# Seven half products in place of eight on a quarter of the depth, in six of the FFN's eleven pairs of blocks

## The reference, cut to what matters

```python
def swiglu(h, w_ffn_in, w_ffn_out):
    gate, up = jnp.split(h @ w_ffn_in, 2, axis=-1)     # h: 256 x 2048, w_ffn_in: 2048 x 11264
    return (jax.nn.silu(gate) * up) @ w_ffn_out         # w_ffn_out: 5632 x 2048

h = rms_norm(x, norm2_gain[l]) * (1 + scale2) + shift2
x = x + gate2 * swiglu(h, w_ffn_in[l], w_ffn_out[l])
```

## Time and profile before

| | |
|---|---|
| median of 3 runs | 3428.91 us |
| profiled execution, whole | 3425.8 us |
| its span, first to last instruction | 3424.1 us |
| mean granted clock of TensorE | 0.875 of full |
| busy over the span | PE 76%, DVE 73%, ACT 25%, POOL 32% |

### The profile page before, as it was taken

One profiled execution on the slowest core, in us unless ns is written; L12 is line 12 of the kernel. 1 busy time (PEld: TensorE's weight loads), 2 busy tenths in 40 slices (PEclk: granted clock), 3 DMA queues, 4 the chain that ended last, 5 costly groups with the idle time before them and its releaser, 6 DMA issues. The chain is left out here.

```text
span 3424.1 us, 27357 instructions
## 1 busy us (share of the span) xinstructions
PE 2587.7 (76%) x10431; PEld 1805.0 (53%) x10431; DVE 2513.7 (73%) x2615; ACT 860.9 (25%) x815; POOL 1102.7 (32%) x654
## 2 busy tenths in 40 slices
PE   9999999616051500035558999999999999999999
PEld 4455774202020200012226888788788788888887
DVE  5987657899999999976776876779566544444565
ACT  2113331100000110000003333455433433333333
POOL 6640007686777688876660000000000000000000
PEclk9999999757575755567779999999999999999999
DMA  8885569999999999999997997455657555555775
GB/s 287 320 315 205 183 243 406 403 422 419 422 421 417 409 420 422 422 421 421 422 421 260 327 323 260 145 162 166 221 185 252 167 194 184 192 187 188 269 266 185
DMA packets 317685, 1023.39 MB, mean 299 GB/s; under 512 B 33656, under 2 KB 34184, under 8 KB 250892
## 3 DMA queue, kind: packets, MB, share of 16 engines
q1 hardware_dynamic: 243676, 484.97, 41.2%
q0 software_dynamic: 73904, 537.04, 37.9%
HBM read 1015.08 MB, written 6.86 MB: 298 GB/s over the span
## 5 line engine op out<-in xcount | busy, mean ns | idle before, releaser
L411 DVE TENSOR_TENSOR slab_low<-ring,slab_high 128x2048 fp32r<-128x2048 f32 x220 | 504.2, 2292 | 488.3 <-ACT slab_high L404 488.2
L404 ACT CAST slab_high<-ring 128x2048 fp32r<-128x2048 f32 x284 | 542.3, 1910 | 890.8 <-PE bank L390 714.7
L2137 POOL DMA_INDIRECT pool<-in_peer_u,pool x237 | 493.8, 2084 | 293.5 <-DVE pool L1861 185.9
L1911 DVE CUSTOM_DVE_ANT_0 pool<-pool,nat 128x2048 f32<-128x2048 f32 x234 | 532.7, 2291 | 45.7 <-DMA pool<-in_peer_u,pool 44.2
L388 PE MATMUL bank<-slab_high,left_high 128*128 128x512 f32 x1408 | 551.3, 392 | 8.4 <-DVE res L1949 3.9
L390 PE MATMUL bank<-slab_high,left_low 128*128 128x512 f32 x1408 | 549.0, 390 | 0.0
L389 PE MATMUL bank<-slab_low,left_high 128*128 128x512 f32 x1408 | 548.8, 390 | 0.0
L2710 PE MATMUL bank<-pool,causal 128*128 128x512 f32 x296 | 181.5, 770 | 415.7 <-ACT causal L2352 325.4
L1922 DVE SCALAR_TENSOR_TENSOR res<-pool,res 128x2048 f32<-128x2048 f32 x169 | 397.4, 2351 | 105.9 <-DMA pool<-in_peer_v,pool 92.5
L2137 POOL DMA_INDIRECT pool<-in_peer_v,pool x242 | 394.9, 1632 | 214.0 <-PE bank L2710 107.7
L2710 PE MATMUL bank<-pool,upto 128*128 128x512 f32 x288 | 195.9, 844 | 209.2 <-DMA pool<-in_peer_v,pool 116.3
(11 more groups left out here) (661 smaller groups left out, 3466.1 us busy)
## 6 DMA issues: line engine op xcount, KB each, us to landing
ring<-in_w_in SPq DMA_DIRECT2D x140, 1024.0 KB, 5.2
ring<-in_w_ffn_in SPq DMA_DIRECT2D x88, 1024.0 KB, 5.0
ring<-in_w_ffn_out SPq DMA_DIRECT2D x44, 1024.0 KB, 5.2
nat<-in_w_ada SPq DMA_DIRECT2D x74, 512.0 KB, 5.8
ring<-in_w_out SPq DMA_DIRECT2D x32, 1024.0 KB, 5.1
ring<-in_w_ada SPq DMA_DIRECT2D x28, 1024.0 KB, 6.7
left_scratch<-in_w_ada SPq DMA_DIRECT2D x38, 512.0 KB, 5.7
pool<-in_w_ada SPq DMA_DIRECT2D x12, 1024.0 KB, 7.1
```

Of the source, the lines that this page charges most:

```text
L404: nc.scalar.copy(high[:, n % PARTS], ring[:, g % SLOTS]).then_inc(high_done, 1)
L411: eng.tensor_tensor(dst, ring[:, g % SLOTS], high[:, n % PARTS].bitcast(F32), ALU.subtract)\
L1911: v.tensor_tensor_reduce(out=row, in0=row, in1=nat[:, t, :], scale=1.0, scalar=0.0, op0=ALU.mult, op1=ALU.add, accum_out=actv[:, t, m:m + ...
L2137: g.indirect_dma_start(dst, None, a[table][0], bass.IndirectOffsetOnAxis(idx[:, t, n:n + 1], 0))\
```

## The change

It applies to pairs 1 to 6 (`SEVEN`). Of each of these pairs, depth quarter 3 (slab (0, 3) of the gate and slab (1, 3) of the up block) is multiplied by Winograd's form of Strassen's scheme. The 2 x 2 blocks are: tokens t x halves of that depth quarter on the left (2 chunks each, `HK`), depth halves x gate/up on the right. Eight half products (6 matmuls each) become seven. The other six slabs (`rest`, r = 0 to 5) stay as before.

- **Left sums, once.** POOL makes four sums of the left's blocks from the normed rows (`left_sums`, 128x256 each); PE transposes them in pair 0 before slab 5 (8 transposes), ACT and DVE split them.
- **Right sums, in each pair.** DVE adds halves of the two slabs in place in the ring (`slab_sum`, four of 128x1024). The parts that PE multiplies are cast and split by halves: FIRST, SECOND, THIRD (two halves each) and FOURTH (one half), seven halves in place of eight, from slots 0 and 1.
- **Order of PE in a pair.** rest 0, FIRST (12 matmuls), rest 1, SECOND (12), hidden transposes, rest 2, THIRD (12), rest 3, FOURTH (6), rest 4, rest 5.
- **Parts.** A third pair of part buffers is laid over the end of `hTh`, which pairs 1 to 6 don't reach. Buffers in that order: 2, 0, 1, 2, 0, 1, 2, 1, 0, 1. FOURTH's cast so waits for THIRD's products, rest 5's for FOURTH's.
- **Banks.** Banks 6 and 7 hold three of the half products in turn. ACT copies FIRST's and SECOND's out (`take`); DVE forms the common sums (`one_and_six`, `with_seventh`, `five_less`), adds them to banks 0 and 1 (`seven_gates`) and 2 and 3 (`seven_ups`). Silu now reads `prod_` in place, after `seven_gates` and after the cast of rest 5 in ACT's queue. Banks 0 and 1 are free for the next pair once `seven_gates` is done.
- **Loads.** Slots 0 and 1 hold the two summed slabs until THIRD's and FOURTH's low parts are made; the loads of rest 4 and rest 5 wait for these. The next pair's first loads stand behind them in SP's queue.
- Some semaphores of the norms are shared, to make room for six new ones; pair 1 is no longer written out by itself.

The diff, cut to its core:

```diff
+        SEVEN, HK = range(1, 7), KS // 2
+        SEVEN_PART = (0, 2, 1, 1)
+        SEVEN_FROM = (((0, 0), (0, 1)), ((1, 1), (0, 0)), ((1, 1), (0, 1)), ((1, 0),))
+        REST_AT, REST_PART, rest_count = (2, 3, 6, 7, 4, 5), (2, 1, 0, 2, 0, 1), (3, 1, 1, 1, 1, 1)
 sync:
-                stream(sp, FFN_IN)
+                ffn_loads()
+                def seven_loads(i):
...
+                    else:
+                        for at, after, p, j in ((2, 5, 0, 0), (3, 6, 0, 1), (0, 7, 0, 3), (1, 8, 1, 3)):
+                            sp.wait_ge(low_done, before + after)
+                            ffn_load(i, at, p, j)
+                    for r in (2, 3):
+                        sp.wait_ge(low_done, before + 8 + r + 1)
+                        ffn_load(i, REST_AT[r], r // 3, r % 3)
+                    for r, last in ((4, THIRD), (5, FOURTH)):
+                        sp.wait_ge(s_wl, i * 4 - 4 + last + 1)
+                        ffn_load(i, REST_AT[r], r // 3, r % 3)
 tensor:
+                def half_product(n, which, lhs, bank, start, stop):
+                    hi, lo = part_pair(SEVEN_PART[n])
+                    for k in range(HK):
+                        lh, ll = lhs(k)
+                        c = HK * which + k
+                        nc.tensor.matmul(ps[bank][:, :], lh, hi[:, c, :], start=start and k == 0, stop=False)
+                        nc.tensor.matmul(ps[bank][:, :], lh, lo[:, c, :], start=False, stop=False)
+                        last = nc.tensor.matmul(ps[bank][:, :], ll, hi[:, c, :], start=False, stop=stop and k == HK - 1)
+                def seven_pair(i, first):
...
+                        pe.wait_ge(s_wd, i * 6 - 7)
+                    rest(i, 0)
+                    pe.wait_ge(s_wl, i * 4 - 3)
+                    half_product(FIRST, 0, own(0, 0), 6, True, True)
+                    half_product(FIRST, 1, own(1, 0), 0, False, False).then_inc(s_wu, 1)
+                    rest(i, 1)
...
+                        pe.wait_ge(s_wd, i * 6 - 6)
+                    pe.wait_ge(s_wl, i * 4 - 2)
+                    half_product(SECOND, 0, summed(3), 2, True, False)
+                    half_product(SECOND, 1, summed(0), 7, True, True).then_inc(s_wu, 1)
...
+                    hidden_transposes(i)
+                    rest(i, 2)
+                    pe.wait_ge(s_wl, i * 4 - 1)
+                    pe.wait_ge(s_wx, i * 2 - 1)
+                    half_product(THIRD, 0, summed(1), 6, True, True)
+                    half_product(THIRD, 1, own(1, 1), 1, False, True).then_inc(s_wu, 1)
+                    rest(i, 3)
+                    pe.wait_ge(s_wl, i * 4 + 0)
+                    pe.wait_ge(s_wx, i * 2 + 0)
+                    half_product(FOURTH, 0, summed(2), 7, True, True).then_inc(s_wu, 1)
+                    rest(i, 4)
+                    rest(i, 5)
 scalar:
+                def seven_silu(i):
+                    act.wait_ge(s_wd, i * 6 - 1)
+                    for t in range(TT):
+                        last = nc.scalar.activation(prod_[:, t, :], prod_[:, t, :], ACT.Silu)
+                    last.then_inc(s_fa, 1)
+                def seven_pair(i, first):
+                    rest_high(i, 0, first)
+                    seven_high(i, FIRST)
+                    rest_high(i, 1)
+                    seven_high(i, SECOND)
+                    rest_high(i, 2)
+                    take(i, FIRST, 6, taken_one)
+                    highs(i - 1)
+                    seven_high(i, THIRD)
+                    rest_high(i, 3)
+                    act.wait_ge(s_fu, i * 1)
+                    take(i, SECOND, 7, taken_five)
+                    seven_high(i, FOURTH)
+                    rest_high(i, 4)
+                    rest_high(i, 5)
+                    seven_silu(i)
 vector:
+                def five_less(i):
+                    dve.wait_ge(s_wx, i * 2 + 0)
+                    dve.wait_ge(s_wd, i * 6 - 4)
+                    v.tensor_tensor(taken_six, taken_five, taken_six, ALU.subtract).then_inc(s_wd, 1)
+                    v.tensor_tensor(taken_five, taken_five, taken_last, ALU.subtract).then_inc(s_wd, 1)
+                def seven_gates(i):
+                    dve.wait_ge(slabs_used, i * 8 + (gf + 5))
+                    dve.wait_ge(s_fT, i * 1)
+                    v.tensor_tensor(prod_[:, 0, :], ps[0][:, :], taken_one, ALU.add)
+                    v.tensor_tensor(prod_[:, 1, :], ps[1][:, :], taken_last, ALU.add).then_inc(s_wd, 1)
+                def seven_pair(i, first):
+                    rest_low(i, 0)
+                    seven_low(i, FIRST)
+                    slab_sum(i, 0, (0, 0), (1, 0))
+                    if first:
+                        product(i - 1)
+                    else:
+                        seven_ups(i - 1)
+                    rest_low(i, 1)
+                    slab_sum(i, 1, (1, 0), (1, 1))
+                    if not first:
+                        seven_product(i - 1)
+                    seven_low(i, SECOND)
+                    slab_sum(i, 2, (1, 1), (0, 0))
+                    slab_sum(i, 3, (0, 1), (1, 1))
+                    rest_low(i, 2)
+                    lows(i - 1)
+                    seven_low(i, THIRD)
+                    rest_low(i, 3)
+                    one_and_six(i)
+                    seven_low(i, FOURTH)
+                    rest_low(i, 4)
+                    with_seventh(i)
+                    rest_low(i, 5)
+                    five_less(i)
+                    seven_gates(i)
```

More of the change, by code:

```diff
@@ L3548, in _, with left_sum_transposes @@
             @block.tensor
             def _(pe):
+                def left_sum_transposes():
+                    pe.wait_ge(s_ws, 4)
+                    pe.wait_ge(s_nl, len(low_order))
+                    for q in range(4):
+                        for j in range(HK):
+                            c = (q % 2 * HK + j) * P
+                            last = nc.tensor.transpose(ps[6 + q // 2][:, c:c + P], summed_rows[q][:, j * P:(j + 1) * P],
+                                                       ident[:, :])
+                    last.then_inc(s_nT, 1)
@@ new lines, in rest @@
+                def rest(i, r):
+                    p, j = divmod(r, 3)
+                    pe.wait_ge(low_done, i * 8 + (nf + sum(rest_count[:r + 1])))
+                    hi, lo = part_pair(REST_PART[r])
+                    for k in range(KS):
+                        for t in range(TT):
+                            lh, ll = left(KS * j + k, t)
+                            o = ps[2 * p + t][:, :]
+                            begin = j == 0 and k == 0 and (p, t) != (1, 0)
+                            end = j == 2 and k == KS - 1 and (p, t) != (0, 1)
+                            nc.tensor.matmul(o, lh, hi[:, k, :], start=begin, stop=False)
+                            nc.tensor.matmul(o, lh, lo[:, k, :], start=False, stop=False)
+                            last = nc.tensor.matmul(o, ll, hi[:, k, :], start=False, stop=end)
+                    last.then_inc(slabs_used, rest_count[r])
@@ L3618, in last_products, with pair @@
                                          j == 0, j == 3)
-                def pair(i, first, second=False):
+                def pair(i, first):
                     for p in range(2):
@@ L3623, in pair @@
                             m = 4 * p + j
+                            if first and p == 1 and j == 1:
+                                left_sum_transposes()
                             if first and p == 0 and j < WHOLE:
@@ L3684, in _ @@
                 pair(0, True)
-                pair(1, False, True)
-                with pe.Fori(2, pairs) as i:
+                seven_pair(SEVEN.start, True)
+                with pe.Fori(SEVEN.start + 1, SEVEN.stop) as i:
+                    seven_pair(i, False)
+                with pe.Fori(SEVEN.stop, pairs) as i:
                     pair(i, False)
@@ L3742, in silu @@
                         act.wait_ge(s_fT, i * 1)
+                    else:
+                        act.wait_ge(s_ws, 2)
                     for t in range(TT):
@@ L3751, in highs, with left_sum_highs, seven_high @@
                     last.then_inc(s_fh, 1)
+                def left_sum_highs():
+                    act.wait_ge(s_nT, len(turn_order) + 1)
+                    for h in range(2):
+                        nc.scalar.copy(summed_high[:, 2 * h:2 * h + 2], view(ps[6 + h][:, :], [2, HK, P])).then_inc(s_nh, 1)
+                def seven_high(i, n):
+                    if n == FIRST:
+                        act.wait_ge(landed[gf % SLOTS], i * 32 + reach[gf])
+                        act.wait_ge(slabs_used, i * 8 + (gf - 1))
+                    elif n == SECOND:
+                        act.wait_ge(landed[(gf + 1) % SLOTS], i * 32 + reach[gf + 1])
+                        act.wait_ge(s_ws, i * 4 + 1)
+                        act.wait_ge(slabs_used, i * 8 + (gf + 3))
+                    elif n == THIRD:
+                        act.wait_ge(s_ws, i * 4 + 4)
```

(50 more changed lines are left out.)

137 lines of the change are left out of this document (122 added, 15 removed).

## The result

The change makes the kernel slower. Its median is 3443.21 us over 7 runs (3441.72 to 3448.71), against 3429.16 for the kernel before (7 runs): +14.1 us, ratio 1.0044, 95% interval 1.0033 to 1.0054. The forecast was +7.7 and 3436.6 us, the range ended at 3443.0: the direction was right, the size too small.

What follows compares the result with a forecast made beforehand. TensorE was taken to bound the kernel. Six times (2.2 + 0.3 - 1.36) gave +6.8, plus 0.9 for the left transposes: +7.7 us, 3436.6 us, with an 8-in-10 range of 3430.5 to 3443.

Steps and rivals of the forecast that it cites:

- The gain of 8.2 us: Six seven-product pairs: six fewer matmuls each on PE, 1.36 us a pair, 8.2 us saved in all.
- the 0.9 us of the left transposes: Pair 0: eight transposes of the left sums on PE, added once, costing 0.90 us.
- Chain 1: From THIRD's products to the next pair's first slab: 19.75 us against PE's 17.68, a 2.2 us stall six times.
- the load that was named: Rest 5's load, on chain 1 after FOURTH's low part: landing takes 5.04 us and releases rest 5's cast.
- Chain 2: From hidden transposes to THIRD: 5.63 us against rest 2's 5.44, with restart 0.3 us in each of six pairs.
- The expected period, 45.6 us: Sign in the changed trace: about 45.6 us between hidden transposes in the six pairs, 44.43 after them.
- The clock falls in the stalls (0.02): Rival, chance 0.02: one slab at 1.2 GHz after each stall adds 33 us, giving 3469.
- DVE's loop to rest 2: DVE's 16.4 us from rest 0's low part ends about 0.9 us before PE needs it: no stall.
- The landing in the burst: Rest 5's load, with two loads behind it, is hardly held up: 5.1 us rather than 5.04.
- POOL beside DVE: POOL's left sums beside DVE's last norm subtractions: price 0 to 0.8 us, taken as 0.

Runs made afterwards that it cites:

- e4: Changed kernel with all pairs plain, keeping only the left sums, their eight transposes and the renamed semaphores: 3430.29 us against 3429.53 before, ratio 1.0000.
- e9: e6 with the next pair's loads for slots 2 and 3 put ahead of rest 4's and rest 5's: 3419.73 us against 3429.48 before, ratio 0.9974.
- e1: Changed kernel with ACT casting the next pair's first slab ahead of the Silus: 3426.78 us against 3429.53 before, ratio 0.9989.
- e3: Changed kernel with rest 5's load bringing one of four chunks, for timing alone: 3434.00 us against 3429.53 before, ratio 1.0012.
- e7: Changed kernel with THIRD's cast and low parts ahead of the hidden rows', Silus left in place: 3439.13 us against 3429.84 before, ratio 1.0027.
- e2: Changed kernel with eight throwaway matmuls in each stall ahead of a pair's first slab: 3438.10 us against 3429.53 before, ratio 1.0026.
- the second measurement: The changed kernel itself run again, 5 runs: 3441.54 us against 3429.84 before, ratio 1.0038.
- e6: Changed kernel with the reorderings of e1 and e7 together, six pairs: 3423.59 us against 3429.84 before, ratio 0.9978.

## Why the prediction was wrong

- **The gain of 8.2 us and the 0.9 us of the left transposes** were right: e4 has +0.90, e9 the whole of the sum, -7.24.
- **Chain 1** was right in place, in each link and in size: forecast 2.07 us late and 0.11 for the restart, measured 1.84 to 2.09 from start to start less one matmul (2.07 to 2.32 less 0.23) and 0.11. e1 took it away with one reordering; e3 moved it by shortening the load that was named.
- **Chain 2** was forecast at 0.30 with its restart; measured are 0.31 to 0.35 of start to start less one matmul, and 0.10 for the restart, so 0.43, in five pairs; in pair 1 the wait is 0.13. e7 gave back 2.1 us for it in six pairs.
- The stretch's 11.3 us less two falls is 8.0, where the sum of these terms said 7.7. The expected period, 45.6 us, was met by four of five.
- **The step that failed is the rival "The clock falls in the stalls (0.02)".** It took one wait of 2.08 us at full clock as evidence that such a wait leaves the clock alone. Six waits of this length came, and behind two of them the clock fell, in each of the three traces with such stalls (the changed kernel twice, e7). The length does not decide which: in the changed kernel it fell behind stalls of 2.21 and 2.16 us from start to start, not behind the one of 2.32. What does decide it is left open. It was not an alternative to the forecast but a term on top of it. Its size was wrong the other way: one fall costs 1.65 us, not a slab at half pace (5.44). So 3.3 us of the 11.3 were missing from the sum. That PE's idle time is the cause is shown by e2: with the same chain and PE kept at work there is no fall.
- The rest of the distance to the measured +14.1, 2.8 us, is not explained by any trace; the second measurement gave +11.7. With +11.3 the range would have held, so both the falls and this rest were needed to leave it, by 0.2 us.
- **DVE's loop to rest 2**, given 0.9 us to spare, was no bound in the changed kernel. **The landing in the burst** was 5.0 for the first of the three loads as forecast, but the same burst is what held e6: the fourth load in a row took 11.7 us. The prediction asked of the burst only what it does to the load on chain 1, not what it does to the loads behind that one.
- **POOL beside DVE** was hidden, as taken: e4 has no more than the transposes' 0.90.

## What to carry to other kernels

When an algorithm saves matmuls in a kernel bound by TensorE, write down each loop of dependences between two products of the engine and compare it with the matmuls in between. The queue order of the other engines decides: here a cast behind two Silus cost more than the six saved matmuls, and moving it gave them back. Price a repeated stall of TensorE with a fall of its clock in some of the places, even where one such stall has left the clock alone. And keep loads that are ready to go from queueing up behind one that is not, or they will land one behind the other later.

## What the runs showed of the hardware

- In three traces with stalls of about 2.0 us (six in each), the granted clock fell behind exactly two of the six, and not always behind the longest; in e3, with six stalls of 1.4 to 1.5 us, behind none; with 1.8 us of each stall filled (e2), behind none.
- A fall costs 1.6 to 1.7 us: matmuls start 0.43 us apart in place of 0.23 for some eight of them.
- Loads of 1 MB on one queue land one behind the other: 5.0, 7.3 and 9.5 us from issue to landing for three issued within 1.0 us (the changed kernel, 2808.1 us); 5.0, 7.3, 10.9 and 11.7 for four, the last 2.9 us after the first (e6, 2760.8 us).
- POOL's sums beside a DVE instruction with two SBUF inputs, in the changed kernel (POOL, then DVE):

```profile
2698.13 0.73 POOL L3618 TENSOR_TENSOR nat<-nat 128x256 f32<-128x256 f32 x1 [409.85 <-DVE nat L4089]
2698.82 2.79 POOL L3619 TENSOR_TENSOR nat<-nat 128x256 f32<-128x256 f32 x1
2701.57 0.73 POOL L3621 TENSOR_TENSOR nat<-nat 128x256 f32<-128x256 f32 x1
```

```profile
2698.57 2.44 DVE L411 TENSOR_TENSOR slab_low<-ring,slab_high 128x2048 fp32r<-128x2048 f32 x1
```

DVE's low part took 2.44 us in place of 2.28, while the POOL sum that began 0.25 us behind it took 2.79 in place of 0.73 and ended 0.60 us behind DVE's. The ten traces with these sums all have 2.44 and 2.79. By the Trainium skill (GPSIMD Engine Reference, Specifications) the two engines contend there. This trace agrees, and here nearly all of the price is POOL's time. It isn't always: in the earlier trace rows DVE's two sums took 5.59 us, where two of that size elsewhere take 2.46.
